# Experts' outputs scaled on leaving PSUM and given back by a selection in two passes; modulation operations singly between subtractions

## The reference, cut to what matters

```python
gate = grp_p[:, None] * jax.nn.softmax(top_val, axis=-1)
expert = grp[:, None] * MOE_EXPERTS_PER_GROUP + top_idx
...
def run_block(args):
    xb, e = args
    hid = jax.nn.silu(xb @ w_gate[e]) * (xb @ w_up[e])
    return hid @ w_down[e]
```

## Time and profile before

| | |
|---|---|
| median of 3 runs | 1438.73 us (1437.88 to 1440.29) |
| the profiled execution, its own time | 1443.45 us |
| its span (first to last instruction) | 1441.7 us |
| PE, matmul | 1305.2 us busy, 91% |
| VectorE | 751.6 us, 52% |
| ScalarE | 453.7 us, 31% |
| mean granted TensorE clock | 0.941 |
| moved from HBM | 352.58 MB, 245 GB/s over the span |

### The profile page before, as it was taken

How to read it: one execution, slowest core, us unless ns; L and a number is a source line. 1 busy time by engine, 2 the same in 40 slices (tenths; PEclk the granted TensorE clock), 3 DMA queues, 4 the chain that set the end, 5 groups by cost and what they waited for, 6 DMA issues and landing times.

```text
span 1441.7 us, 16421 instructions
## 1 busy us (share of the span) xinstructions
PE 1305.2 (91%) x6222; PEld 893.8 (62%) x6222; DVE 751.6 (52%) x1447; ACT 453.7 (31%) x733; POOL 25.0 (2%) x60
## 2 busy tenths in 40 slices
PE   4979999998996889999995995779999999999995
PEld 4877788876775677888764984654444444444442
DVE  3675977776757568777765997531111111111113
ACT  3424444444534244444443652311100110001001
POOL 0000000000000000000002000000000000000000
PEclk8989999999996599999997998879999999999998
DMA  7337777544430247775531320579799999999992
GB/s 260 119 123 292 271 265 254 194 175 152 144 136 1 88 164 276 262 251 213 202 120 59 118 88 0 207 323 420 294 401 428 431 429 429 430 432 431 430 428 93
DMA packets 114009, 354.37 MB, mean 246 GB/s; under 512 B 6858, under 2 KB 62851, under 8 KB 97698
## 3 DMA queue, kind: packets, MB, share of 16 engines
q1 hardware_dynamic: 107474, 327.96, 58.0%
q0 software_dynamic: 6336, 25.17, 4.7%
q10 hardware_dynamic: 144, 0.52, 0.1%
HBM read 352.58 MB, written 1.05 MB: 245 GB/s over the span
## 4 chain that ended last, share of the span: by engine, by line
PE 75%; DVE 17%; ACT 3%; DMA 3%; SPq 1%; issue 1%; DVEq 0%; ACTq 0%
PE ps L2431 15%; PE ps L397 13%; PE ps L399 12%; PE ps L398 12%; PE ps L2460 7%; DVE xn L2076 4%; PE ps L2420 4%; PE ps L2469 4%; DVE w_lo L371 2%; DMA odd_expert<-in_moe_w_up 1%; DMA dense_weights<-in_ev_w_in 1%; PE ps L929 1%; SPq L1010 1%; DVE ada_acc L1899 1%; PE ps L1665 1%
## 5 line engine op out<-in xcount | busy, mean ns | idle before, releaser
L371 DVE TENSOR_TENSOR w_lo<-dense_weights,w_hi 128x1024 fp32r<-128x1024 f32 (+1 forms) x228 | 270.3, 1208 | 136.8 <-ACT w_hi L366 136.5
L366 ACT CAST w_hi<-dense_weights 128x1024 fp32r<-128x1024 f32 (+1 forms) x228 | 234.3, 1041 | 280.1 <-PE ps L399 245.3
L397 PE MATMUL ps<-w_hi,xT_lo 128*128 128x512 f32 (+1 forms) x624 | 253.3, 406 | 32.9 <-DVE xT_lo L2111 9.4
L398 PE MATMUL ps<-w_lo,xT_hi 128*128 128x512 f32 (+1 forms) x624 | 247.9, 397 | 0.0
L399 PE MATMUL ps<-w_hi,xT_hi 128*128 128x512 f32 (+1 forms) x624 | 247.7, 397 | 0.0
L397 PEld LDWEIGHTS ps<-w_hi,xT_lo 128*128 128x128 f32 x624 | 121.7, 195 | 64.2 <-issue 15.8
L399 PEld LDWEIGHTS ps<-w_hi,xT_hi 128*128 128x128 f32 x624 | 121.1, 194 | 25.9
L398 PEld LDWEIGHTS ps<-w_lo,xT_hi 128*128 128x128 f32 x624 | 121.8, 195 | 24.3 <-issue 0.2
L2549 DVE COPY ge_y<-ps 128x512 f32<-128x512 f32 x32 | 22.1, 692 | 198.3 <-PE ps L2460 198.3
L2460 PE MATMUL ps<-dense_weights,ge_hidT 128*64 128x512 f32 x256 | 115.0, 602 | 0.8 <-ACT ge_hidT L2512 0.8
L2431 PE MATMUL ps<-dense_weights,ge_xT 128*64 128x512 f32 x512 | 112.7, 592 | 1.2 <-ACT ge_xT L2501 1.2
(11 more groups left out here) (384 smaller groups left out, 1723.5 us busy)
## 6 DMA issues: line engine op xcount, KB each, us to landing
dense_weights<-in_moe_w_gate SPq DMA_DIRECT2D x16, 2048.0 KB, 12.8
dense_weights<-in_moe_w_up SPq DMA_DIRECT2D x16, 2048.0 KB, 17.2
dense_weights<-in_moe_w_down SPq DMA_DIRECT2D x16, 2048.0 KB, 10.7
odd_expert<-in_moe_w_gate SPq DMA_DIRECT2D x15, 2048.0 KB, 15.3
odd_expert<-in_moe_w_up SPq DMA_DIRECT2D x15, 2048.0 KB, 19.8
odd_expert<-in_moe_w_down SPq DMA_DIRECT2D x15, 2048.0 KB, 15.3
ada_w<-in_ada_w POOLq DMA_DIRECT2D x12, 2048.0 KB, 8.6
dense_weights<-in_w_gate SPq DMA_DIRECT2D x22, 1024.0 KB, 7.3
```

The source lines that it names most:

```text
L366: act.copy(split_view(w_hi, name, i, j), piece(name, i, j)).then_inc(hi_ready, 1)
L371: dve.tensor_tensor(split_view(w_lo, name, i, j), piece(name, i, j), split_view(w_hi, name, i, j).bitcast(F32), ALU.subtract).then_inc(pie ...
L397: pe.matmul(out, left[1], right[0], start=start, stop=False)
L398: pe.matmul(out, left[0], right[1], start=False, stop=False)
```

## The change

In the experts' stage the share is taken out of the matmul that gives the outputs back. ScalarE's copy of the turned shares also sums them per place into `ge_gate` (each place has one token, so the sum is that token's share), and no longer waits for the give-back before. VectorE makes `ge_selT` from `ge_shareT`: 1 where it is above 0. The output leaves PSUM in two steps, for each half of the columns: ScalarE writes it times `ge_gate`, rounded to fp32r (`y_high`), then VectorE the rest, output times `ge_gate` less that (`y_low`). `give_back` multiplies the selection with both, as fp32r, 8 matmuls instead of 4. Some tiles move into memory of others that are free by then.

In the feed-forward stages `ada_products` becomes `ada_part`, which does some of the ten operations. Five slots in each step of blocks 1 to 10 take one each, and two each in block 1 and block 10; so blocks 1 and 10 hold a whole modulation block, and the pairs 2-3, 4-5, 6-7 and 8-9 one each. Block 0 holds none.

```diff
-                ge_a = st("ge_a", [P, BLK])
-                ge_hid = st("ge_hid", [P, 2, BLK])
-                ge_hidT = st("ge_hidT", [P, 2, 2, P])
                 ge_shareT = st("ge_shareT", [P, T, P])
-                ge_y = st("ge_y", [P, 2, 512])
+                ge_selT = st("ge_selT", [P, T, P], F32R)
+                ge_y_hi = st("ge_y_hi", [P, 2, 512], F32R)
+                ge_y_lo = st("ge_y_lo", [P, 2, 512], F32R)
...
+        ge_hid = g_v[:].rearrange("p (e f) -> p e f", e=2)
+        ge_hidT = g_mh[:].rearrange("p (e c n) -> p e c n", e=2, c=2)
+        ge_gate = ms[:, 32:33]
+        ge_a = cmask[:, 2 * T * EXPERTS:]
...
+                def ada(n, slot, it):
+
+                    if n >= 1:
+                        block, first, each = (n // 2, 0, 2) if n in (1, FF_BLOCKS - 1) else (n // 2, n % 2 * 5, 1)
+                        ada_part(dve, ADA_PER_LAYER * self.layer + block, range(first + each * slot, first + each * (slot + 1)), it)
+
                 def step(n, it):
-                    self.splits(dve, split_lo, n, it, (0, 1, 2))
+                    self.splits(dve, split_lo, n, it, (0,))
+                    ada(n, 0, it)
+                    self.splits(dve, split_lo, n, it, (1,))
+                    ada(n, 1, it)
+                    self.splits(dve, split_lo, n, it, (2,))
                     if n >= 1:
                         copy(n - 1, it)
+                    ada(n, 2, it)
                     self.splits(dve, split_lo, n, it, (3,))
                     for t in range(T):
                         dve.wait_ge(self.tanh, self.count(n, it, T) + t + 1)
@@ -890,9 +904,10 @@
                         dve.wait_ge(self.gate_half_made, self.count(n, it, T) + t + 1)
                         dve.scalar_tensor_tensor(out=ff_hid[:, t], in0=ff_a[:, t], scalar=rstd[:, 2, t:t + 1],
                                                  in1=ps[:, t, BLK:2 * BLK], op0=ALU.mult, op1=ALU.mult).then_inc(self.hid, 1)
-                    self.splits(dve, split_lo, n, it, (4, 5))
-                    if n in ADA_AT:
-                        ada_products(dve, ADA_PER_LAYER * self.layer + ADA_AT.index(n), it)
+                    self.splits(dve, split_lo, n, it, (4,))
+                    ada(n, 3, it)
+                    self.splits(dve, split_lo, n, it, (5,))
+                    ada(n, 4, it)
 
...
+        def ada_part(dve, j, ops, it):
+
+
+            for k in ops:
+                if k < KC:
+                    w, c_col = ada_w[:, j % ADA_BUFFERS, k], c_act[:, k:k + 1]
+                    if k == 0:
+                        dve.wait_ge(ada_landed[j % ADA_BUFFERS], per_round(16 * (j // ADA_BUFFERS + 1), it, 16))
+                        ins = dve.tensor_scalar(ada_acc[:], w, c_col, None, ALU.mult)
+                    else:
+                        dve.wait_ge(ada_steps, per_round(KC * j + k, it, 2 * KC))
+                        ins = dve.scalar_tensor_tensor(out=ada_acc[:], in0=w, scalar=c_col, in1=ada_acc[:], op0=ALU.mult, op1=ALU.add)
+                    ins.then_inc(ada_steps if k < KC - 1 else ada_used, 1)
+                elif k == KC:
+                    dve.wait_ge(ada_used, per_round(j + 1, it, 2))
+                    dve.transpose(ada_accT[:], ada_acc[:]).then_inc(ada_steps, 1)
                 else:
-                    dve.wait_ge(ada_steps, per_round(KC * j + k, it, 2 * KC))
-                    ins = dve.scalar_tensor_tensor(out=ada_acc[:], in0=w, scalar=c_col, in1=ada_acc[:], op0=ALU.mult, op1=ALU.add)
-                ins.then_inc(ada_steps if k < KC - 1 else ada_used, 1)
-            dve.wait_ge(ada_used, per_round(j + 1, it, 2))
-            dve.transpose(ada_accT[:], ada_acc[:]).then_inc(ada_steps, 1)
-            dve.wait_ge(ada_steps, per_round(KC * (j + 1), it, 2 * KC))
-            n = ADA_COLS // 32
-            sums = mod_parts[:, bass.ds(per_round(n * j, it, 2 * n), n)]
-            dve.tensor_reduce(sums, ada_accT[:].rearrange("p (b i) -> p b i", i=32), AX.X, ALU.add).then_inc(ada_parts, 1)
+                    dve.wait_ge(ada_steps, per_round(KC * (j + 1), it, 2 * KC))
+                    n = ADA_COLS // 32
+                    sums = mod_parts[:, bass.ds(per_round(n * j, it, 2 * n), n)]
+                    dve.tensor_reduce(sums, ada_accT[:].rearrange("p (b i) -> p b i", i=32), AX.X, ALU.add).then_inc(ada_parts, 1)
...
                     for n in range(2):
                         pe.wait_ge(self.y, at(2 * p + n + 1, it, 2))
                         for t in range(T):
-                            last = pe.matmul(ps[:, 4 + 2 * t + n, :], ge_shareT[:, t], ge_y[:, n],
-                                             start=(p == 0), stop=(p == self.PAIRS - 1))
+                            pe.matmul(ps[:, 4 + 2 * t + n, :], ge_selT[:, t], ge_y_lo[:, n], start=(p == 0), stop=False)
+                            last = pe.matmul(ps[:, 4 + 2 * t + n, :], ge_selT[:, t], ge_y_hi[:, n],
+                                             start=False, stop=(p == self.PAIRS - 1))
                         if n == 0 and p == self.PAIRS - 1:
...
@@ -2500,22 +2518,29 @@
                     act.wait_ge(self.gathered, at(p + 1, it, 1))
                     act.copy(ge_xT[:], ps[:, 2:4, :].rearrange("p b (k n) -> p (b k) n", k=4)).then_inc(self.xT, 1)
 
+                def y_high(p, it):
+
+                    for n, made in enumerate((self.half_down, down_used)):
+                        act.wait_ge(made, at(p + 1, it, 1))
+                        act.activation(ge_y_hi[:, n], ps[:, n, :], ACT.Copy, scale=ge_gate).then_inc(self.y_high, 1)
+
                 def step(p, it):
+                    if p > 0:
+                        y_high(p - 1, it)
                     for e in range(2):
                         act.wait_ge(gu_used, at(2 * p + e + 1, it, 2))
                         act.activation(ge_th[:, e], ps[:, 2 + e, 0:BLK], ACT.Tanh, scale=0.5).then_inc(self.tanh, 1)
                     act.wait_ge(self.share_turned, at(p + 1, it, 1))
-                    if p > 0:
-                        act.wait_ge(self.given, at(p, it, 1))
-                    act.copy(ge_shareT[:], ps[:, 1, 0:T * P].rearrange("p (t n) -> p t n", t=T)).then_inc(self.copied, 1)
+                    act.activation(ge_shareT[:], ps[:, 1, 0:T * P].rearrange("p (t n) -> p t n", t=T), ACT.Copy, accum_out=ge_gate).then_inc(self.copied, 1)
                     act.wait_ge(self.turned, at(p + 1, it, 1))
-                    act.copy(ge_hidT[:], ps[:, 0, :].rearrange("p (e c n) -> p e c n", e=2, c=2)).then_inc(self.copied, 1)
+                    act.copy(ge_hidT, ps[:, 0, :].rearrange("p (e c n) -> p e c n", e=2, c=2)).then_inc(self.copied, 1)
                     if p < self.PAIRS - 1:
                         copy_x(p + 1, it)
 
                 def gathered():
                     copy_x(0, None)
                     self.pairs(act, step)
+                    y_high(self.PAIRS - 1, None)
 
                 self.either(act, gathered, lambda: self.all_tokens.act(act))
...
@@ -2543,23 +2568,30 @@
                         last = dve.tensor_scalar(ge_share[:, t, cut], places, where, share, ALU.is_equal, ALU.mult)
                     last.then_inc(self.share, 1)
 
-                def copy_y(p, it):
-                    for n, made in enumerate((self.half_down, down_used)):
-                        dve.wait_ge(made, at(p + 1, it, 1))
-                        dve.tensor_copy(ge_y[:, n], ps[:, n, :]).then_inc(self.y, 1)
+                def turned_selection(p, it):
+                    dve.wait_ge(self.copied, at(2 * p + 1, it, 2))
+                    if p > 0:
+                        dve.wait_ge(self.given, at(p, it, 1))
+                    dve.tensor_scalar(ge_selT[:], ge_shareT[:], 0.0, None, ALU.is_gt)
+
+                def y_low(p, it):
+                    for n in range(2):
+                        dve.wait_ge(self.y_high, at(2 * p + n + 1, it, 2))
+                        dve.scalar_tensor_tensor(out=ge_y_lo[:, n], in0=ps[:, n, :], scalar=ge_gate, in1=ge_y_hi[:, n].bitcast(F32),
+                                                 op0=ALU.mult, op1=ALU.subtract).then_inc(self.y, 1)
 
                 def hidden(p, it, e):
                     n = at(2 * p + e + 1, it, 2)
                     dve.wait_ge(self.tanh, n)
-                    dve.scalar_tensor_tensor(out=ge_a[:], in0=ge_th[:, e], scalar=1.0, in1=ps[:, 2 + e, 0:BLK], op0=ALU.add,
+                    dve.scalar_tensor_tensor(out=ge_a, in0=ge_th[:, e], scalar=1.0, in1=ps[:, 2 + e, 0:BLK], op0=ALU.add,
                                              op1=ALU.mult).then_inc(self.half, 1)
                     dve.wait_ge(self.half, n)
-                    dve.tensor_tensor(ge_hid[:, e], ge_a[:], ps[:, 2 + e, BLK:2 * BLK], ALU.mult).then_inc(self.hid, 1)
...
                 def step(p, it):
                     if p > 0:
-                        copy_y(p - 1, it)
+                        y_low(p - 1, it)
                     else:
```

(28 more changed lines are left out.)

1 line of the change is left out of this document (added).

## The result

The changed kernel takes 1429.26 us (median of 10 runs, 1425.37 to 1435.3) against 1439.51 for the kernel before (10 runs, 1437.13 to 1443.88): a ratio of 0.9927, 95% interval [0.9909, 0.9944], so 8.1 to 13.1 us faster. The forecast was 1434.8 us, with a range from 1431.5 to 1438.2: the right side, but a gain of 3.9 us where the medians show 10.2. The profiled execution took 1429.31 us (span 1427.6) against 1443.45, 14.1 less; that of the kernel before lay some 4 us above the median.

What follows compares the result with a forecast made beforehand. PE set the pace, but in the experts' stage transfers were slower by 0.3 us a pair; 5.7 (experts) - 0.1 (feed-forward) - 1.7 (clock) = 3.9 us off the 1438.73 median gave 1434.8, range 1431.5 to 1438.2.

Steps and rivals of the forecast that it cites:

- The experts' term: Experts' stage: faster give-backs, held back by the weight transfers, save 5.7 us in all.
- Last gate/up: Final expert pair: the last odd gate/up group starts at 1401.3 instead of 1406.59, 5.3 us earlier.
- The stream: Experts' weight transfers: they end 2.5 us earlier, between 1.7 and 3.4.
- The first hole: Transfer gap between 1013 and 1017 us, early in the experts' stage: ends 1.7 us earlier.
- the second: Transfer gap between 1045 and 1053 us, DMA share 0.77: returns 0 to 1.7 us, taken as 0.8.
- Waits from the sixth pair on: Experts' stage: PE idles some 2 us ahead of each odd gate/up group, until its up weights land.
- The tail: End of the experts' stage: gating begins 1.55 instead of 1.94 us after the final down group, 0.4 gained.
- The feed-forward term: Feed-forward stages: 1.76 us saved behind block 0 of layer 0, 1.9 lost at the layers' ends, net -0.1.
- The lumps: Feed-forward stages before: ten DVE modulation operations together, 7.3 us, claimed to hold PE only behind block 0.
- the lateness at the layer's end: End of each feed-forward layer: added modulation operations in the last block make PE resume 0.95 us later, 1.9 for both.
- The clock: Two layer ends and the experts' final pair: one fall of PE's clock expected, costing 1.7 us (0 to 5.1).
- Rival (b): Whole kernel: no fall of PE's clock, or a larger one-off transfer gain, giving 1432.2 to 1433.1 us; chance 0.27.

Runs made afterwards that it cites:

- e1: The kernel before with the experts' edit alone, keeping the old modulation lumps: 1432.49 us, ratio 0.9959 to the kernel before.
- f4: The changed kernel with the modulation operations in lumps of ten again, none behind block 0, the last behind the last low half: 1440.75 us, ratio 0.9999.
- g1: The changed kernel with the last four modulation operations of block 10 moved behind the last low half: 1427.76 us, ratio 0.9934 to the kernel before.
- g2: As g1, plus eight unused 512-column matmuls on PE ahead of block 1 of each feed-forward stage: 1425.07 us, ratio 0.9910 to the kernel before.
- e2: The kernel before with the feed-forward edit alone, keeping the old give-back: 1434.47 us, ratio 0.9975 to the kernel before.
- f3: The kernel before, fetching only half of the rows of the down weights from the fourth pair on: 1440.27 us, ratio 0.9987 to the kernel before.
- e3: The changed kernel run again unchanged, on the chip of the two single-edit kernels: 1430.44 us, ratio 0.9955 to the kernel before.

## Why the prediction missed

**The experts' term, 5.7 us: right.** Last gate/up 5.3 earlier, forecast; 5.0 in the profile, and 4.9 to 6.6, 5.7 in the mean, in the seven profiles that have the changed stage whole (the changed kernel three times, e1, f4, g1 and g2). The stream: the up weights of expert 31 land 444.62 instead of 447.08 behind the stage's start, 2.5 earlier as forecast (2.4 to 4.0 over the seven). The first hole gave 1.8 of it (1.7 forecast) and the second at most 1.1 (0.8 forecast; the 8 x 0.23 of the forecast is 1.8, not 1.9, which changes nothing). Waits from the sixth pair on, 1.8 instead of 2.0, because a pair takes PE 27.36 and not 27.2. The tail gave 0.44 for 0.4. e1's 5.3 to 5.9 in the medians is this term. Of the Trainium skill's two ceilings, in DMA: Bandwidth & Descriptors, section Where 436 GB/s comes from, the 430 and 431 GB/s of the changed kernel again lie just below the 435 and well above the 358 that the page says binds transfers from HBM; here the measurement decides, and the 358 did not bind.

**The feed-forward term, -0.1: the step that failed.** "The lumps did not hold PE except behind block 0" was read from idle times. First, PE's starts show 0.2 lost in each of three later blocks and 0.1 in each of two more, 0.8 a layer: 1.6. Second, behind block 0 the time from turn to turn falls from 19.03 to 16.81 in layer 0, 2.2 and not 1.76, since the wait's edges cost too. Third, in layer 1 I counted 0 because the fall of the clock had hidden the lump; not quite: 0.65 remained from turn to turn (17.46 against 16.81). And with the lump gone an execution in which the clock stays up is shorter still: layer 1 of e2, with no fall, is 2.55 shorter than that of before. Fourth, the lateness at the layer's end is 0.55 of wait (0.7 to the addition), not 0.95: DVE had the operations done earlier than by adding them to its last idle time. Together 3.3 us in this profile and 5.0 in e2's. One thing more lies in e1 and f3, which have the lump behind block 0: the clock fell behind the 1.76 too, and from turn to turn layer 0 took 20.52 and 20.51 instead of 19.03. So the price of that wait, too, varies from execution to execution. Block 0 to 1 is shorter by 2.5 in layer 0 and 1.1 in layer 1 if the three profiles with that lump are averaged against the nine with the edit and without the eight matmuls, 3.6 where the pair of profiles has 3.1.

**The clock, -1.7: it didn't come.** Waits of 1.95 at a layer's end were followed by a fall in 1 of 12 cases (layer 0 of e3, 14.69 instead of 13.06). In the final pair the fall was already there before: that group takes 8.79 in the kernel before and in e2 and 7.09 in f3, 7.10 in five of the nine profiles with the changed stage and the old final order, and 8.5 to 8.8 in four. For this pair I had charged an additional fall to waits that were not new. In the pair of profiles it even counts 1.7 the other way; over all of them it is a few tenths at most.

So of the missing 6.3 us (10.2 measured in the medians of that comparison, less 3.9), 3.4 are the feed-forward stages and 1.7 the clock. The rest, 1.2, is within the interval of the ratio; 0.5 and 0.4 of it are what the means over all profiles add to the first blocks and to the experts' stage, but neither is clear of the scatter. The 3.6 us of untouched stages in the two profiles belong to the scatter too: the profiled execution of before lay 4 above its median. Rival (b), no fall of the clock, was right in its mechanism and still ended 3 us too high, by the same step.

## What to carry to other kernels

Before a gain on the busiest engine is counted, compare its period with the period of whatever feeds it, here 28.94 against 29.24: beyond the slower one only the lead and the tail are won. Where a profile calls an engine 100% busy, compare the distances of its starts with the best pitch seen elsewhere, since many waits of a tenth stand in no idle column. Where a short wait is unavoidable and recurs, filling it with useless matmuls can be cheaper than the clock that it costs. When a stretch is compared before and after a change, count both from the start of their stage: in the same microseconds of the two traces a hole can seem closed that has only moved.

## What the runs showed of the hardware

Behind an idle time of 2.26 us of PE, the same to a hundredth, the granted clock fell in 11 of 18 cases of the changed schedule; behind 1.95 in 1 of 12, behind 1.40 ahead of a layer's last down group in none of 16, and behind 0.45 at block 1 in none of 4. The length alone doesn't decide: behind the waits of 1.8 for up weights in the experts' stage it fell in 28 of 57 cases over nine profiles, more often than behind 1.95, and behind the 1.76 to 1.79 in layer 0 of the three profiles with the lump in 2 of 3. Why is open. Such a fall costs 1.4 to 1.7 us, and nothing where the next wait is for a transfer at full rate: the weights' time to landing shrank from 21.5 to 19.8 us. Eight fp32r matmuls of 128x512 between fp32 groups start 0.23 to 0.24 apart, behind a first one of 0.33.
